# A two-block sequence model on one core: who writes the gate table's zeros, and who scales the residual

## The reference

```
first block:  h = h + [gated delta net, forgetting attention](rmsnorm(h)) @ w_out
              h = h + swiglu(rmsnorm(h))          # feed-forward, width 2816
              x = rmsnorm(h, final_norm_w)        # handed to the second block
second block: mod = silu(c) @ ada_w + ada_b       # six vectors of 1024
              h = modulate(rmsnorm(x)); q, k, v, cb, cc, cu = h @ w_in
              x = x + gate1 * ([window attention, short conv] @ w_out)
              h2 = modulate(rmsnorm(x))
              x = x + gate2 * peer(h2)            # 8 heads x 16 of 16384 experts per token
peer:         a = u_tab @ h2;  out = (gates * gelu(a)) @ v_tab, gates zero but at the chosen experts
```

## Time and profile before

| | |
|---|---|
| median of 3 runs | 2426.67 us (2423.17 to 2426.86) |
| the profiled execution | 2427.28 us, span 2425.5 us (first to last instruction) |
| mean granted TensorE clock | 0.99 of full speed |
| busy: PE, DVE, ACT, POOL | 2390.9, 1435.7, 874.2, 1045.5 us |
| HBM read, written | 364.28 MB, 61.05 MB |

### The profile page before, as it was taken

How to read it: one execution, slowest core, us unless ns; L and a number is a source line. 1 busy time by engine, 2 the same in 40 slices (tenths; PEclk the granted TensorE clock), 3 DMA queues, 4 the chain that set the end, 5 groups by cost and what they waited for, 6 DMA issues and landing times.

```text
span 2425.5 us, 33627 instructions
## 1 busy us (share of the span) xinstructions
PE 2390.9 (99%) x11435; PEld 1464.0 (60%) x11435; DVE 1435.7 (59%) x2831; ACT 874.2 (36%) x1385; POOL 1045.5 (43%) x739
## 2 busy tenths in 40 slices
PE   8999899999999999999999999999999999999999
PEld 6888677658888875445454444444444466666665
DVE  4412455456867556544949894222222399999988
ACT  3222223232232242223135655544544433333332
POOL 0001111010000020000888888888888175578666
PEclk9999889999999999999999999999999999999999
DMA  7240100265656312942436666666666799999997
GB/s 207 70 72 1 53 10 10 70 178 156 191 176 205 87 53 70 345 174 87 87 48 153 154 148 153 155 147 154 155 147 156 257 401 375 370 361 375 374 361 287
DMA packets 437701, 426.49 MB, mean 176 GB/s; under 512 B 104809, under 2 KB 359913, under 8 KB 437489
## 3 DMA queue, kind: packets, MB, share of 16 engines
q1 hardware_dynamic: 353456, 332.85, 43.0%
q0 software_dynamic: 84160, 92.58, 15.5%
HBM read 364.28 MB, written 61.05 MB: 175 GB/s over the span
## 4 chain that ended last, share of the span: by engine, by line
PE 96%; DVE 2%; ACT 1%; SPq 0%; issue 0%; DMA 0%; POOL 0%; DVEq 0%; ACTq 0%; POOLq 0%
PE psum L1474 9%; PE psum L1475 9%; PE psum L1476 9%; PE psum L1499 7%; PE psum L1497 7%; PE psum L1498 7%; PE psum L1249 6%; PE psum L889 6%; PE psum L1206 5%; PE psum L1208 5%; PE psum L1207 5%; PE psum L1455 4%; PE psum L1106 1%; PE psum L1083 1%; PE psum L1062 1%; PE psum L1122 1%
## 5 line engine op out<-in xcount | busy, mean ns | idle before, releaser
L786 POOL DMA_INDIRECT dense_gates<-arena x384 | 607.2, 1581 | 151.6 <-issue 116.7
L1474 PE MATMUL psum<-arena 128*128 128x512 bf16 x1024 | 389.4, 380 | 0.0
L1476 PE MATMUL psum<-arena 128*128 128x512 bf16 x1024 | 387.1, 378 | 0.0
L1475 PE MATMUL psum<-arena 128*128 128x512 bf16 x1024 | 386.6, 378 | 0.0
L2545 DVE TENSOR_TENSOR arena<-arena,psum 128x1024 bf16<-128x1024 f32 x124 | 151.5, 1221 | 352.2 <-ACT psum L1855 351.7
L1498 PE MATMUL psum<-arena,low 128*128 128x384 bf16 x1024 | 333.8, 326 | 0.0
L1499 PE MATMUL psum<-arena,low 128*128 128x384 bf16 x1024 | 333.8, 326 | 0.0
L1497 PE MATMUL psum<-arena,low 128*128 128x384 bf16 x1024 | 333.8, 326 | 0.0
L1871 ACT ACTIVATE low<-low 128x1024 bf16<-128x1024 f32 x128 | 135.3, 1057 | 296.3 <-PE psum L1499 282.6
L814 POOL DMA_INDIRECT arena<-gelu_spill,arena x128 | 178.3, 1393 | 87.5 <-DMA gelu_spill<-cst 43.3
L806 POOL DMA_INDIRECT arena<-in_v,arena x128 | 166.3, 1300 | 103.0 <-DVE arena L2592 77.5
(11 more groups left out here) (377 smaller groups left out, 3937.0 us busy)
## 6 DMA issues: line engine op xcount, KB each, us to landing
arena<-in_uT SPq DMA_DIRECT2D x128, 512.0 KB, 4.6
low<-in_v SPq DMA_DIRECT2D x128, 512.0 KB, 5.3
gelu_spill<-cst SPq DMA_DIRECT2D x128, 256.0 KB, 3.4
arena<-in_ada_w POOLq DMA_DIRECT2D x12, 2048.0 KB, 9.3
dense_gates<-arena SPq DMA_DIRECT2D x4, 6144.0 KB, 40.1
arena<-gelu_spill SPq DMA_DIRECT2D x128, 192.0 KB, 5.2
arena<-dense_gates SPq DMA_DIRECT2D x128, 192.0 KB, 6.7
low<-in_w_in SPq DMA_DIRECT2D x20, 1024.0 KB, 7.4
```

Of the source, the lines that this page charges most:

```text
L786: pool.indirect_dma_start(gate_cells, bass.IndirectOffsetOnAxis(ap=cell_of[:, n:n + 1], axis=0), gate_of[:, n:n + 1], None, compute_op=ALU ...
L1474: mm(psum[:, bank, :], hi[:, c, :], h2hi[:, c, :], start=c == 0, stop=False)
L1475: mm(psum[:, bank, :], hi[:, c, :], h2lo[:, c, :], start=False, stop=False)
L1476: last = mm(psum[:, bank, :], lo[:, c, :], h2hi[:, c, :], start=False, stop=c == DC - 1)
```

## The change

1. `zeros` is no strip of its own any more but the first 384 columns of `kf`, a scratch row of the table of sines and cosines, which has been read when `tab` reaches 1. GpSimd clears it after the load of strip 6 of `ada_w`.
2. The zeros are issued by GpSimd in sixteen transfers of 8 rows (1.57 MB) instead of four by SP: two behind each load of strips 8 to 11, and the other eight behind the last.
3. `last_norm` leaves VectorE. VectorE announces the reciprocal with an empty instruction, and GpSimd multiplies all of `xT2` (128 x 8 x 512) by `col_ln` and then by `r2[:, 1]`, in place.
4. VectorE waits for all sixteen clears before the window attention, and for the second multiplication (`x2_ready` 3) before `res2`.

```
+        zeros = kf[:, 0:DEN]
-        zeros = carve(DEN)
+        top[0] += DEN
...
-            sp.wait_ge(S["pool_step"], 10)
-            for q in range(4):
-                sp.dma_start(io["dense"][q * 32:(q + 1) * 32, :, 0:DEN].rearrange("i j t -> j i t"),
-                             zeros.unsqueeze(1).to_broadcast([P, 32, DEN])).then_inc(S["zeroed"], 16)
...
+            def clear(q):
+                pool.dma_start(io["dense"][q * 8:(q + 1) * 8, :, 0:DEN].rearrange("i j t -> j i t"),
+                               zeros.unsqueeze(1).to_broadcast([P, 8, DEN])).then_inc(S["zeroed"], 16)
...
             for k in range(2, MODS * P // MOD_W):
                 pool.wait_ge(S["mod_acc"], k - 1)
                 load_ada(k)
+                if k == 6:
+                    pool.wait_ge(S["tab"], 1)
+                    step(pool.memset(zeros, 0.0))
+                elif k > 7:
+                    pool.wait_ge(S["pool_step"], 10)
+                    clear(2 * k - 16)
+                    clear(2 * k - 15)
+            for q in range(8, 16):
+                clear(q)
...
-            pool.wait_ge(S["x2_ready"], DC)
-            step(pool.memset(zeros, 0.0))
+            pool.wait_ge(S["x2_ready"], 1)
+            pool.tensor_tensor(xT2, xT2, col_ln[:, 0:DC].unsqueeze(2).to_broadcast([P, DC, SEC]), ALU.mult
+                               ).then_inc(S["x2_ready"], 1)
+            pool.wait_ge(S["x2_ready"], 2)
+            pool.tensor_tensor(xT2, xT2, r2[:, 1, :].unsqueeze(1).to_broadcast([P, DC, SEC]), ALU.mult
+                               ).then_inc(S["x2_ready"], 1)
...
-            pool.wait_ge(S["zeroed"], 64)
+            pool.wait_ge(S["zeroed"], 256)
...
-            def last_norm(c):
-                stt(xT2[:, c, :], xT2[:, c, :], col_ln[:, c:c + 1], r2[:, 1, :], ALU.mult, ALU.mult).then_inc(S["x2_ready"], 1)
+            dve.engine_nop().then_inc(S["x2_ready"], 1)
...
-                if j < 4:
-                    last_norm(2 * j)
-                    last_norm(2 * j + 1)
...
+            dve.wait_ge(S["zeroed"], 256)
             for s in range(SC * KV):
...
                 dve.wait_ge(S["out2_done"], f + 1)
+                dve.wait_ge(S["x2_ready"], 3)
```

## The result

The changed kernel takes **2447.11 us** in the median (2443.27 to 2449.42), the kernel before on the same chip 2426.77: a ratio of 1.0085 (95% interval 1.0071 to 1.0100), 20.3 us slower. The prediction was 2428.6 us, with a range from 2424.5 to 2441. The profiled execution took 2447.78 us, 20.5 more than that of before.

The account below looks back on a forecast made before the run. TensorE, busy 99% of the span, was taken to bound the kernel. All terms were 0 except 1.9 us at the first rotation: 2427.28 + 1.9 = 2429.2, adjusted by 0.6 towards the median to 2428.6 us; range 2424.5 to 2441.

Parts of the forecast that it names:

- Sixteen clears on GpSimd: In the feed-forward, issuing and moving the clears beside strips and weights was to cost 0, bounds 0 to 2.5 us.
- If the queues take turns by transfer: Premise in the feed-forward: strip 11 done at 785.8 and landed at 786.4 us, just in time, so 0.
- a rival: Feed-forward: queues served packet by packet, 20.5 us a pair, weights fall back some 13 us: 2442 us; chance 0.10.
- Zeros out of SP's queue: Behind the projections: removing four issues and 25.2 MB where TensorE does not wait gains 0.
- Eight `last_norm` off VectorE: Second block's projections to output product: VectorE saves 5.6 us, TensorE gains 0, at most 2.5 us.
- Two multiplications on GpSimd: At the first rotation: the second multiplication holds VectorE's scaling of the queries, so TensorE waits 1.9 us.
- the worst case: At the first rotation: second multiplication of 10.6 us, TensorE stands 8 us, clock drop 1.7 us, 9.7 in all; chance 0.07.
- The new waits: Before the window attention and `res2`: clears end before 860 us, the multiplication 160 us earlier than wanted; both cost 0.
- Strip 11: Sign in the feed-forward: strip 11 would be used within 3 us of 787.

Follow-up runs that it names:

- both mends: The change with clears issued one at a time and its two multiplications cut into sixteen of 128x512, against the kernel before: 2426.26 us against 2425.97, ratio 1.0004.
- The short multiplications: The kernel before, zeros still by SP, with last_norm moved to GpSimd as sixteen multiplications of 128x512: 2426.44 us against 2427.27, ratio 0.9993.

## Why the prediction was wrong

**The failed step** is "*Sixteen clears on GpSimd* ... I take 0; 0 to 2.5", and in it the premise "If the queues take turns by transfer". It cost 14.6 us. With that premise I priced only the landing of strip 11, and put what the clears do to the weights of the feed-forward at nothing; the queues took turns by packet instead, and the weights' pair took 24.0 us. The premise came from a window that was 2 us too early. I read from the earlier trace rows that weights issued at 758.48 had no packet from 760 to 762 us, and held it against alternation by packet. In the next window of the kernel before, 762 to 764 us, both queues are there:

```profile
q0 software_dynamic: 179, 0.72, 92.9%
q1 hardware_dynamic: 126, 0.06, 11.4%
```

The weights' first packets come some 4 us behind their issue, and from then on about as many as the strip's. The strip ended soon after (23 packets from 764 to 766 us), so before the change the effect lasted for two us and nobody waited. The Trainium skill (DMA: Bandwidth & Descriptors, "Queues, rings and completion order") states that an engine goes round its queues packet by packet; the trace agrees, 1709 to 1708. I had that as a rival, with 13 us of delay and 2442 us, and gave it 0.10. Its mechanism was right. Its 13 us come near the 14.6 of the feed-forward, in part by luck: they rest on an estimated packet of 3072 bytes and 20.5 us a pair, where 4254 bytes and 24.0 us were measured, and how they follow from the pair's time was not worked out.

The other steps:
- *Zeros out of SP's queue*, 0: right. With both mends the time is that of before, and the zeros by GpSimd in the old place cost nothing either.
- *Eight `last_norm` off VectorE*, 0: right. The short multiplications free VectorE just as much and give 0.9993.
- *Two multiplications on GpSimd*: the mechanism was right in place and kind, the term mis-sized. It says 1.9 us; 4.33 us were measured. The second multiplication took 8.83 us, not 7.5, which with the smaller parts put the end of the hold 1.0 us later, counted from GpSimd's start. And TensorE came to the rotation 1.5 us sooner, as the half clock behind the wait of 2.9 us did not occur this time (granted 1.00 in the row below, 0.58 in the earlier trace rows). The drop of the clock behind the new wait, which the prediction kept for the worst case alone, came with it. So the term was 5.6 us (the stretch of 72.18 us against 66.55), inside its bounds of 0 to 9.7.
- *The new waits*, 0: right. The clears' last 316 packets went after 820 us, at some 85 a us, and none between 826 and 830, so all were done by about 825 us, long before VectorE asks for them.
- Strip 11 was used at 791.18 us, not at 787, but behind VectorE's wait of 6.01 us for ScalarE's split, which ended at 788.57, not for its own transfer: it is the weights that were late.

The window of after behind its wait of 2.9 us, which ended at 901.20:

```profile
901.00:905.00 4.00, 3.81 (x18) 3.39 (x19) 3.96 (x8) 2.84 (x8) 0.00 (x0) 1.00 0.01 4
```

Without the failed step the terms as measured would give 2427.3 + 5.6 - 0.6, some 2432 us, inside the range.

## What to carry to other kernels

Here two queues took turns one packet to one, so a bulk write with packets of 4254 bytes left a stream of prefetches with packets of 512 some 11% of the bytes for as long as it lasted. Ask how many packets of each queue have to be served, not how many bytes fit, and space bulk writes so that the prefetches catch up between them; in this kernel one clear behind every split was enough. Cut an operation that is handed to GpSimd into pieces no longer than the slack of the VectorE instructions beside it: the hold was 7 us beside one piece of 4096 elements and 1.0 us beside pieces of 512. Before a view of 2 us is taken for a rule, read the next ones.

## What the hardware showed that I had not expected

- An engine that issues into a hardware queue can stand there: SP for 20.33 us in one issue, ScalarE for 17.19 us in four of 1024 pieces each. That the queue was full then is argued from the weights' slow turns, not shown.
- The first packets of weights issued at 758.48 us, while GpSimd's strip filled the engines, appeared between 762 and 764 us; the turns one to one began only then. What delays the first of them is open.
- GpSimd's multiplication by a row broadcast over the chunks takes 8.83 us for 4096 elements (2.16 ns an element), by a column 7.02 (1.71). In pieces of 512 they take 8.03 and 10.30 us for eight, whatever holds by VectorE's instructions fell into them included.
- The half clock behind a wait is not fixed to it: behind the same wait of 2.9 us the granted clock was 0.58 in one execution and 1.00 in another. Where a term is below 2 us, this alone can double it or take it away.
